# A gate's products as three rounded ones, and a projection's weights loaded after the recurrence

## The chip, the cores and the metric

The kernel runs on one core of a Trainium2 chip. The metric is the device time of one execution in microseconds (us).

## The reference, cut to what matters

One transformer block with 512 tokens of width 1024: a mixer with two branches, then a mixture of experts.

```python
p = h @ w_in                                     # h: 512 x 1024
q, k, v, rw_cols, gate_logits = split(p)
y_sb = stick_breaking_attention(q, k, v)         # 512 x 512
y_rw = rwkv7_time_mix(rw_cols, ...)              # 512 x 512, a recurrence over the tokens
g_sb, g_rw = split(sigmoid(gate_logits + gate_bias))   # 512 x 1024 each
merged = g_sb * (y_sb @ w_o_sb) + g_rw * (y_rw @ w_o_rw)
x = x + gt1 * rmsnorm(merged @ w_out, gain)
# then: h = rmsnorm(x)...; x = x + gt2 * rmsnorm(experts(h), gain)
```

The change touches the logits of the second gate, `h @ w_in[:, gate columns of g_rw]`, and the projection `y_rw @ w_o_rw`.

## The kernel before

Everything is laid out by hand: each engine has its own list of instructions, and they wait for one another on counting semaphores. Values are kept transposed, with features on the 128 partitions and the 512 tokens along the free axis. `arena` is 17 slots of 128x2048 float32, `ring` has three places of 128x4096 for weights on their way, and tensors of other names (`h_upper`, `wo1_upper`, ...) are laid over the same memory, so that one slot has many tenants in turn. Slots 15 and 16 hold `hT`, the transposed h, in 8 pieces of 128x512 (KD = 8). Slots 0, 1 and 4 hold the tokens of the recurrence, slots 3, 7 and 14 its small matrices.

**Weights** come over the queue of SP in the order of `chunk_table`; each chunk has a place and waits until the chunk that had the place before is used up (`used_by`). GR0 to GR3 are four chunks of 1 MB of gate weights, each for two tiles of 128 columns, in halves of the ring's second place, where `w_o_sb` (OSB) was before. `w_o_rw` (two loads of 1 MB, `load_orw`) goes into two arena slots, just ahead of GR2. WO1 and WO0 are the halves of w_out.

**Two kinds of product.** Most products are full precision: float32 on both sides. Others are written as three products of rounded operands (type fp32r): a value is the sum of an upper part, rounded by a copy into fp32r (ScalarE for weights and h, GpSimd for w_o_rw), and a lower part, value minus upper part (a subtraction on GpSimd or VectorE), and the product is upper x upper + lower x upper + upper x lower. The first projections (L1550 to L1552), the w_o_rw products (L1877 to L1879) and the output products (L1908 to L1910) are made so. The gates (L1656) are full precision.

**The order around the change:**

- Attention with the products of the first gate (GS), then the 64x64 triangular inverses of the recurrence's 8 chunks, with the attention output (w_o_sb, L1667, read out by ScalarE at L843) as filler. Its last product frees the place of GR0 and GR1.
- The start states: products L1798, copied out by ScalarE (L862), the first of them copied on by VectorE to `Zs` (L1222).
- The recurrence, 8 chunks in order (`for cc in range(NCH)`). In each, TensorE forms the z products (L1816), VectorE adds (L1226), TensorE forms the sa products (L1823), ScalarE copies them (L879), TensorE forms outputs and the next state (L1841, L1849), VectorE updates the state (L1235, L1238) and ScalarE copies the outputs (L883). Ahead of each of three of these steps stands `gate_part`, two of the GR products, six in a chunk: 48 of the 64. ScalarE reads out each finished gate tile (`gate_evac`, L873).
- The tail: a group norm over each head (sums L1855 and L1862 on TensorE, squares, logarithm and exponential L895 to L899 on ScalarE, L1242 to L1248 on VectorE), with the last 16 GR products between and behind L1862. Then y is rounded (ScalarE, L902) and its lower part formed (VectorE, L1251), GpSimd rounds and splits the second half of w_o_rw (L580, L582), and TensorE forms the w_o_rw products, output tile by output tile (f = 0 to 7, four k in each).
- VectorE multiplies by the gates and adds (L1262, L1263), the sum is split (L914, L1256), w_out is split (ScalarE L908, GpSimd L587), the output products follow in two halves of four token tiles, ScalarE squares each bank (L923, L927), then comes the norm, the router, and a loop over the experts, whose weights (w_up, w_down) SP loads.

The wait at the head of the w_o_rw products is for each k of the first tile: its lower part of y and its parts of w_o_rw.

Of the kernel before, what the change touches and what calls it, by code (L numbers as in the profile page):

```python
# [20 lines left out]
P = 128  # L21
# [96 lines left out]
def build(nc, x, c, w_mod, b_mod, gains, w_in, gate_bias, shift_mu, w0, w_decay_up, a0, w_iclr_up, w_gate_up,  # L118
# [3 lines left out]
    with ctx:  # L122
# [20 lines left out]
        with (nc.sbuf_tensor("over0", [P, 4096], F32), nc.sbuf_tensor("wo0_lower", [P, KD, 512], F32R) as wo0_lower,  # L143
              nc.sbuf_tensor("over1", [P, 4096 + 1024], F32), nc.sbuf_tensor("m_upper0", [P, 6, 512], F32R) as m_upper0,
              nc.sbuf_tensor("over2", [P, 7 * 2048], F32), nc.sbuf_tensor("wo0_upper0", [P, 4, 512], F32R) as wo0_upper0,
              nc.sbuf_tensor("over3", [P, 2048], F32), nc.sbuf_tensor("wo0_upper1", [P, 4, 512], F32R) as wo0_upper1,
              nc.sbuf_tensor("over4", [P, 2048], F32), nc.sbuf_tensor("m_upper1", [P, 2, 512], F32R) as m_upper1,
              nc.sbuf_tensor("over5", [P, 3072], F32), nc.sbuf_tensor("wo1_upper", [P, KD, 512], F32R) as wo1_upper):
            pass
        with (nc.sbuf_tensor("on0", [P, 3 * 4096 + 2 * 2048], F32), nc.sbuf_tensor("orw_upper0", [P, 2, D], F32R) as orw_upper0,  # L150
              nc.sbuf_tensor("on1", [P, 5 * 2048], F32), nc.sbuf_tensor("orw_upper1", [P, 2, D], F32R) as orw_upper1,
              nc.sbuf_tensor("on2", [P, 2048], F32), nc.sbuf_tensor("y_lower", [P, FT, T], F32R) as y_lo,
              nc.sbuf_tensor("on3", [P, 3 * 2048], F32), nc.sbuf_tensor("orw_lower1", [P, 2, D], F32R) as orw_lower1):
            pass
# [35 lines left out]
        def S4(i):  # L190
# [14 lines left out]
        s_orw = (11, 14)  # L205
# [8 lines left out]
               for i in (s_MT, s_X, s_XT, s_Mak, s_Mrb, s_Mrk, s_W, s_B, s_Kd)}  # L214
# [17 lines left out]
        m_hi = [m_upper0[:, k, :] for k in range(6)] + [m_upper1[:, k, :] for k in range(2)]  # L232
        m_lo = [w_parts[:, :, :, :, :].rearrange("p a b k n -> p (a b k n)")[:, 512 * k:512 * k + 512] for k in range(KD)]
        wo_hi = [[wo1_upper[:, k, :] for k in range(KD)],
                 [wo0_upper0[:, k, :] for k in range(4)] + [wo0_upper1[:, k, :] for k in range(4)]]
# [134 lines left out]
        orw_hi = [orw_upper0[:, k, :] for k in range(2)] + [orw_upper1[:, k, :] for k in range(2)]  # L370
        orw_lo = [wo0_upper1[:, 2 * k:2 * k + 2, :].rearrange("p a n -> p (a n)") for k in range(2)]
        orw_lo += [orw_lower1[:, k, :] for k in range(2)]
        W_SPLIT, H_SPLIT, H_ROUNDED = len(proj_tiles) + FT, KD // 2 + FT, KD + FT
# [49 lines left out]
        def load_orw(eng):  # L423

            eng.wait_ge(hp_done, 4)
# [8 lines left out]
        def _(sp):  # L434
            sp.wait_ge(params_in, 16 * N_SMALL)
            for n, (name, src, width, sl) in enumerate(chunk_table):
# [14 lines left out]
                if name == "GR2":  # L451
                    load_orw(sp)
                if name == "WO1":
                    sp.wait_ge(yc_done, NCH)
                    sp.wait_ge(zc_evac, NCH)
                if name == "WO0":
                    sp.wait_ge(sb_gated, KD)
                    sp.wait_ge(rows_moved, 16)
                    for m in range(4):
                        if m in (0, 3):  # L460
                            sp.dma_start(rows[:, 0, :] if m == 0 else row_out, mod_dram[m, :].partition_broadcast(P)).then_inc(rows_moved, 16)
# [6 lines left out]
            sp.wait_ge(mix_done, 4 * KD)  # L468
            load_expert(sp, 1, 0, 1)
# [68 lines left out]
        def _(pool):  # L538
# [35 lines left out]

            pool.wait_ge(orw_in, 32)
            for k in range(FT):
                if k == 2:
                    pool.wait_ge(yc_done, NCH)
                whole_k = orw[k // 2][:, k % 2, :]
                nc.gpsimd.tensor_copy(orw_hi[k], whole_k).then_inc(h_split[0], 1)  # L580
                pool.wait_ge(h_split[0], KD // 2 + k + 1)
                nc.gpsimd.tensor_tensor(orw_lo[k], whole_k, orw_hi[k].bitcast(F32), ALU.subtract).then_inc(w_split, 1)  # L582

            def output_weight_lower(half, k):

                pool.wait_ge(w_rounded, len(proj_tiles) + KD * half + k + 1)
# [7 lines left out]
            nc.gpsimd.memset(S(14), 0.0)  # L594
            nc.gpsimd.memset(S(13)[:, D:2 * D], 0.0).then_inc(hrow_zero, 1)
            pool.wait_ge(merged_ready, KD)
            nc.gpsimd.memset(none, 0.0).then_inc(hrow_zero, 1)

            pool.wait_ge(hrow_zero, 1)
# [53 lines left out]
        def _(act):  # L653
# [203 lines left out]

            for b in range(4):
# [9 lines left out]
            act.dma_start(mod_dram.rearrange("m (f p) -> (m f) p", p=P), prow[0:32, :]).then_inc(rows_moved, 16)  # L868

# [19 lines left out]

            act.dma_start(x1[:, :, :], x.rearrange("o (t p) n -> p (o t) n", p=P)).then_inc(x_in, 16)  # L890
# [113 lines left out]
        def _(dve):  # L1004
# [211 lines left out]
            PCv = PC[:, :].rearrange("p (f c) -> p f c", c=NCH)  # L1216
            f4 = lambda a: a.rearrange("p (f v) -> p f v", f=FT)
            pairs = lambda a: a.rearrange("p (g b v) -> p g b v", b=2, v=HD)
            for cc in range(NCH):
                if cc == 0:  # L1220
                    dve.wait_ge(hp_evac, 8)
                    CP(Zs[:, :], tok[s_H][:, 0, :, :].rearrange("p f v -> p (f v)")).then_inc(zc_evac, 1)  # L1222
                else:
# [25 lines left out]
            for f in range(FT):  # L1249
                dve.wait_ge(h_rounded, KD + f + 1)  # L1250
# [212 lines left out]
        def _(pe):  # L1463
# [180 lines left out]
            def gate(branch, n, ks, bank):  # L1644
# [10 lines left out]
                for k in ks:  # L1655
# [211 lines left out]
            for f in range(KD):  # L1867
# [4 lines left out]
                for k in range(FT):  # L1872
                    if f == 0:
                        pe.wait_ge(h_split[1], KD // 2 + k + 1)
                        pe.wait_ge(w_split, len(proj_tiles) + k + 1)
# [188 lines left out]
```

## Time and profile before

| | us |
|---|---|
| median of 3 runs (lowest, highest) | 1157.81 (1157.76 to 1158.61) |
| profiled execution, own time | 1158.76 |
| its span | 1157.0 |
| TensorE busy | 1019.7 (88%) |
| TensorE loading weights | 540.0 (47%) |
| VectorE busy | 399.9 (35%) |
| ScalarE busy | 275.7 (24%) |
| GpSimd busy | 207.9 (18%) |
| mean granted clock of TensorE, share of full | 0.97 |

The busy times are unions over one profiled execution, so an engine's share is an average over stages with different limits. PE is TensorE, PEld its weight loads, DVE VectorE, ACT ScalarE, POOL GpSimd, SP the engine whose queue issues the loads. The records of the tile names are those of the memory, so a name can be that of another tenant.

### The profile page before, as it was taken

How to read it: one execution, taken by the hardware profiler on the slowest of the kernel's cores; microseconds unless marked ns; L12 is line 12 of the kernel's file. 1: busy time of each engine (PE TensorE's matmuls, PEld its weight loads, DVE VectorE, ACT ScalarE, POOL GpSimd, SP SyncE). 2: the span in 40 equal slices, each digit the busy share in tenths (PEclk: the TensorE clock that was granted, in tenths of full speed). 3: DMA queues.
4: the chain of work that ended last, by engine and by line, in shares of the span. 5: the costliest groups of instructions: out<-in, count | busy, mean ns of one | idle time of the engine just before them, and what ended most of it. 6: DMA issues, size and time to landing. Idle time of an engine off the chain costs nothing.

```text
span 1157.0 us, 16874 instructions
## 1 busy us (share of the span) xinstructions
PE 1019.7 (88%) x7002; PEld 540.0 (47%) x7002; DVE 399.9 (35%) x822; ACT 275.7 (24%) x435; POOL 207.9 (18%) x246
## 2 busy tenths in 40 slices
PE   3899999999998999999998799987777778878886
PEld 1578644465555676555886433333223232323231
DVE  1322466455557443115726412211111111111014
ACT  2343350066552222216433000000000000000004
POOL 0345200003330100102710121111111111111002
PEclk9599999999999999999999799999999999899999
DMA  8434314343322002314527999999999999999995
GB/s 326 158 123 149 106 40 145 139 152 110 109 73 74 3 4 76 111 38 178 208 106 284 343 399 401 393 397 405 406 410 405 406 406 411 392 400 402 412 412 226
DMA packets 71186, 281.67 MB, mean 243 GB/s; under 512 B 9754, under 2 KB 19244, under 8 KB 46554
## 3 DMA queue, kind: packets, MB, share of 16 engines
q1 hardware_dynamic: 63408, 265.94, 59.3%
q0 software_dynamic: 5120, 8.40, 2.3%
q10 hardware_dynamic: 2602, 6.52, 1.5%
q8 instruction: 43, 0.70, 0.3%
q14 instruction: 13, 0.11, 0.0%
HBM read 276.62 MB, written 12.60 MB: 250 GB/s over the span
## 4 chain that ended last, share of the span: by engine, by line
PE 49%; SPq 30%; DVE 7%; DMA 7%; ACT 4%; issue 2%; POOL 1%; ACTq 0%; POOLq 0%; DVEq 0%
SPq L410 21%; PE ps L1656 7%; SPq L414 5%; PE ps L1537 5%; PE ps L1978 4%; SPq L418 3%; PE ps L1550 2%; PE ps L1667 2%; DMA ring<-in_w_up 2%; PE ps L1551 2%; PE ps L1552 2%; PE ps L1582 2%; PE ps L1993 2%; DMA ring<-in_w_mod 2%; PE ps L1766 1%
## 5 line engine op out<-in xcount | busy, mean ns | idle before, releaser
L1978 PE MATMUL ps<-arena 128*64 128x512 f32 x672 | 151.8, 596 | 34.9 <-DMA arena<-in_w_up 34.9
L1423 DVE TENSOR_TENSOR arena<-arena,ps 128x256 f32<-128x256 f32 x32 | 13.5, 421 | 371.1 <-ACT arena L961 371.1
L1656 PE MATMUL ps<-arena,ring 128*128 128x512 f32 x256 | 118.6, 604 | 0.2 <-DMA ring<-in_w_in 0.2
L1978 PEld LDWEIGHTS ps<-arena 128*64 128x64 f32 x672 | 48.9, 137 | 136.4 <-issue 105.2
L1993 PE MATMUL ps<-arena 128*64 128x512 f32 x336 | 83.4, 641 | 19.4 <-DMA arena<-in_w_down 14.8
L1978 PE MATMUL ps<-ring,arena 128*64 128x512 f32 x352 | 80.5, 601 | 14.8 <-DMA ring<-in_w_up 14.8
L961 ACT ACTIVATE arena<-ps 128x256 f32<-128x256 f32 x32 | 12.3, 384 | 259.4 <-PE ps L1978 259.4
L1656 PEld LDWEIGHTS ps<-arena,ring 128*128 128x128 f32 x256 | 46.1, 190 | 49.1 <-issue 47.2
L1418 DVE TENSOR_SCALAR arena<-ps,par 128x64 f32<-128x64 f32 x256 | 67.2, 334 | 4.1 <-PE ps L1967 4.1
L558 POOL TENSOR_SCALAR_AFFINE_SELECT arena<-arena 128x128 f32<-128x128 f32 x64 | 32.4, 540 | 186.3 <-DVE arena L1149 168.5
L968 ACT ACTIVATE arena<-ps 128x512 f32<-128x512 f32 x32 | 19.1, 597 | 187.8 <-PE ps L1993 187.8
L629 POOL COPY dst_now<-dst_i 128x1 int32 x27 | 4.8, 178 | 300.5 <-ACT arena L968 300.5
L1978 PEld LDWEIGHTS ps<-ring,arena 128*64 128x64 f32 x352 | 26.8, 138 | 66.7 <-issue 39.1
L1993 PEld LDWEIGHTS ps<-arena 128*64 128x64 f32 x336 | 26.4, 146 | 61.9 <-issue 44.9
L1537 PE MATMUL ps<-arena,ring 128*128 128x512 f32 x128 | 55.1, 592 | 0.0
L1993 PE MATMUL ps<-ring,arena 128*64 128x512 f32 x176 | 43.6, 641 | 11.0 <-DMA ring<-in_w_down 8.7
L542 POOL TENSOR_TENSOR w_parts<-ring,w_parts 128x1024 fp32r<-128x1024 f32 (+1 forms) x15 | 38.6, 2578 | 80.8 <-ACT w_parts L701 80.8
L1550 PE MATMUL ps<-h_upper,w_parts 128*128 128x512 f32 (+1 forms) x120 | 48.1, 401 | 4.4 <-ACT arena L709 4.4
L1551 PE MATMUL ps<-h_lower,w_parts 128*128 128x512 f32 (+1 forms) x120 | 47.8, 398 | 0.0
L1552 PE MATMUL ps<-h_upper,w_parts 128*128 128x512 f32 (+1 forms) x120 | 47.7, 397 | 0.0
L1967 PEld LDWEIGHTS ps<-cst,arena 64*128 64x128 f32 x256 | 30.7, 201 | 32.1 <-issue 32.1
L1967 PE MATMUL ps<-cst,arena 64*128 64x64 f32 x256 | 35.0, 278 | 5.4 <-DMA arena<-h_rows,idx_i 5.4
(377 smaller groups left out, 1584.1 us busy)
## 6 DMA issues: line engine op xcount, KB each, us to landing
arena<-in_w_up SPq DMA_DIRECT2D x84, 1024.0 KB, 28.9
ring<-in_w_up SPq DMA_DIRECT2D x44, 1024.0 KB, 28.8
ring<-in_w_down SPq DMA_DIRECT2D x11, 2048.0 KB
arena<-in_w_down SPq DMA_DIRECT2D x11, 2048.0 KB, 32.3
ring<-in_w_mod SPq DMA_DIRECT2D x10, 2048.0 KB, 9.1
arena<-in_w_down SPq DMA_DIRECT2D x20, 1024.0 KB
ring<-in_w_in SPq DMA_DIRECT2D x6, 2048.0 KB, 8.4
ring<-in_w_in SPq DMA_DIRECT2D x8, 1024.0 KB, 9.0
```

The lines of the kernel that those rows point to most:

```text
L410: eng.dma_start(eset_up[u][i][:, 2048 * m:2048 * m + 2048], src).then_inc(w_in_sem[u][m], 16)
L414: eng.dma_start(dst, src).then_inc(w_in_sem[u][m], 16)
L542: nc.gpsimd.tensor_tensor(w_parts[:, n % 2, 1, :, 0:w], chunk(name, KD)[:, :, a:a + w], w_parts[:, n % 2, 0, :, 0:w].bitcast(F32), ALU.sub ...
L1418: last = TS(hgT[:, k, :], ps[:, 0, CAP * k:CAP * k + CAP], V("A1", k), V("SH1", k), ALU.mult, ALU.add)
L1537: last = mm(ps[0:m_, b, :], w[:, k, a:a + m_], hT[:, k, :], start=(k == 0), stop=(k == KD - 1))
L1550: mm(ps[0:m_, b, :], hi, h_hi[:, k, :], start=(k == 0), stop=False)
L1551: mm(ps[0:m_, b, :], hi, h_lo[:, k, :], start=False, stop=False)
L1552: last = mm(ps[0:m_, b, :], lo, h_hi[:, k, :], start=False, stop=(k == KD - 1))
L1656: last = mm(ps[:, bank, :], w[:, k, P * (n % 2):P * (n % 2) + P], hT[:, k, :], start=(k == 0), stop=(k == KD - 1))
L1967: last = tr(ps[:, 0, CAP * k:CAP * k + CAP], hv[:, k, :], ident[0:CAP, 0:CAP])
L1978: last = mm(ps[64 * hf:64 * hf + 64, UP_BANK[u], :].rearrange("p (m n) -> p m n", m=2), hgT[:, k, :], up_pair(u, k)[:, :, 256 * hf:256 * h ...
L1993: last = mm(ps[64 * hf:64 * hf + 64, DOWN_BANK[u], :], hv2[:, k % 2, k // 2, :], wd[:, k % 2, 512 * hf:512 * hf + 512], start=(k == 0), st ...
```

## The change

1. The products of the second gate, 64 in full precision, become 192 rounded ones. The first gate (GS) stays.
2. h is split once more: ScalarE rounds its 8 rows into `g_upper0` and `g_upper1` (slots 11 and 14), four before the start states are copied out and four after it; the lower parts overwrite `hT`, even rows on GpSimd, odd ones on VectorE around the copy of Zs.
3. The gate weights are split tile by tile: ScalarE rounds 128x1024 into one of two halves of slot 2, GpSimd subtracts in place. Tiles 0 and 1 are rounded around the start states, tile n+2 after tile n is read out. GpSimd makes all of these ahead of its work on w_o_rw.
4. `w_o_rw` goes to slots 0 and 1, which the recurrence uses to its end. It is loaded behind the waits for the end of the recurrence, ahead of WO1. GpSimd rounds and splits all four parts after that.
5. x is loaded a second time after the w_o_rw products and no longer when the recurrence has ended; the first of the late rows is loaded there too. The clearing of slot 14 follows the output products.

The core of the diff (memory overlays, renumbered waits and places left out):

```diff
                 if name == "AQ":
...
-                if name == "GR2":
-                    load_orw(sp)
                 if name == "WO1":
                     sp.wait_ge(yc_done, NCH)
                     sp.wait_ge(zc_evac, NCH)
+                    load_orw(sp)
...
             sp.wait_ge(mix_done, 4 * KD)
+            sp.dma_start(rows[:, 0, :], mod_dram[0, :].partition_broadcast(P)).then_inc(rows_moved, 16)
             load_expert(sp, 1, 0, 1)
...
+            def gate_rows_lower(k):
+                pool.wait_ge(h_rounded, KD + k + 1)
+                nc.gpsimd.tensor_tensor(g_lo[k], hT[:, k, :], g_hi[k].bitcast(F32), ALU.subtract).then_inc(h_split[0], 1)
+            def gate_weight_lower(n):
+                pool.wait_ge(w_rounded, len(proj_tiles) + n + 1)
+                at = slice(P * (n % 2), P * (n % 2) + P)
+                nc.gpsimd.tensor_tensor(gw_lo[n // 2 % 2][:, :, at], chunk(f"GR{n // 2}", KD)[:, :, at], gw_hi[n % 2].bitcast(F32),
+                                        ALU.subtract).then_inc(w_split, 1)
+            gate_rows_lower(0)
+            gate_rows_lower(2)
+            gate_weight_lower(0)
+            gate_rows_lower(4)
+            gate_rows_lower(6)
+            for n in range(1, KD):
+                gate_weight_lower(n)
             pool.wait_ge(orw_in, 32)
+            pool.wait_ge(yc_done, NCH)
             for k in range(FT):
-                if k == 2:
-                    pool.wait_ge(yc_done, NCH)
                 whole_k = orw[k // 2][:, k % 2, :]
                 nc.gpsimd.tensor_copy(orw_hi[k], whole_k).then_inc(h_split[0], 1)
...
             act.wait_ge(dve_chunk, 8)
+            def gate_rows_upper(k):
+                A(g_hi[k], hT[:, k, :], ACT.Copy).then_inc(h_rounded, 1)
+            def gate_weight_upper(n):
+                arrived(act, f"GR{n // 2}")
+                if n >= 2:
+                    act.wait_ge(mix_done, 2 * KD + n - 1)
+                A(gw_hi[n % 2], chunk(f"GR{n // 2}", KD)[:, :, P * (n % 2):P * (n % 2) + P], ACT.Copy).then_inc(w_rounded, 1)
+            for k in range(4):
+                gate_rows_upper(k)
+            gate_weight_upper(0)
             for b in range(4):
...
+            for k in range(4, KD):
+                gate_rows_upper(k)
+            gate_weight_upper(1)
...
                         gate_evac(n)
-            act.dma_start(x1[:, :, :], x.rearrange("o (t p) n -> p (o t) n", p=P)).then_inc(x_in, 16)
+                        gate_weight_upper(n + 2)
...
-                if k == 4:
+                if k == 0:
                     act.wait_ge(mix_done, 4 * KD)
+                    act.dma_start(x1[:, :, :], x.rearrange("o (t p) n -> p (o t) n", p=P)).then_inc(x_in, 16)
...
-                for k in ks:
+                if branch == "GR":
+                    cols = slice(P * (n % 2), P * (n % 2) + P)
+                    if ks[0] == 0:
+                        pe.wait_ge(w_split, len(proj_tiles) + n + 1)
+                    for k in ks:
+                        if n == 0:
+                            pe.wait_ge(h_rounded, KD + k + 1)
+                            pe.wait_ge(h_split[k % 2], KD // 2 + k // 2 + 1)
+                        mm(ps[:, bank, :], gw_hi[n % 2][:, k, :], g_hi[k], start=(k == 0), stop=False)
+                        mm(ps[:, bank, :], gw_hi[n % 2][:, k, :], g_lo[k], start=False, stop=False)
+                        last = mm(ps[:, bank, :], gw_lo[n // 2 % 2][:, k, cols], g_hi[k], start=False, stop=(k == KD - 1))
+                for k in ks if branch == "GS" else ():
                     last = mm(ps[:, bank, :], w[:, k, P * (n % 2):P * (n % 2) + P], hT[:, k, :], start=(k == 0), stop=(k == KD - 1))
```

## Rows read from the trace of the kernel before

**Rows 1.** The page: busy share of the DMA engines in 40 slices, and the chain by line.

```profile
DMA  8434314343322002314527999999999999999995
...
SPq L410 21%; PE ps L1656 7%; SPq L414 5%; PE ps L1537 5%; PE ps L1978 4%; SPq L418 3%; PE ps L1550 2%; PE ps L1667 2%; DMA ring<-in_w_up 2%; PE ps L1551 2%; PE ps L1552 2%; PE ps L1582 2%; PE ps L1993 2%; DMA ring<-in_w_mod 2%; PE ps L1766 1%
```

**Rows 2.** Timeline of one step of the recurrence, VectorE and TensorE: start, duration, engine, line.

```profile
500.58 0.43 DVE L1226 TENSOR_TENSOR SDZ<-ps,arena 128x256 f32<-128x256 f32 x1 [1.97 <-PE ps L1816]
...
502.36 0.46 PE L1823 MATMUL ps<-SDZ,arena 64*64 64x64 f32 x15
```

**Rows 3.** Timeline of TensorE: first gate products, the tail, the fourth w_o_rw product.

```profile
458.73 3.70 PE L1656 MATMUL ps<-arena,ring 128*128 128x512 f32 x8 [0.24 <-DMA ring<-in_w_in]
...
532.02 1.02 PE L1862 MATMUL ps<-arena,cst 128*128 128x512 f32 x2
...
532.88 11.32 PE L1656 MATMUL ps<-arena,ring 128*128 128x512 f32 x26
...
546.10 0.39 PE L1877 MATMUL ps<-wo_upper,orw_upper 128*128 128x512 f32 x1
```

**Rows 4.** Timeline of ScalarE in the output stage: one square for each bank.

```profile
577.49 0.60 ACT L923 ACTIVATE arena<-ps 128x512 f32<-128x512 f32 x1 [4.18 <-PE ps L1910]
...
582.93 0.60 ACT L923 ACTIVATE arena<-ps 128x512 f32<-128x512 f32 x1 [4.42 <-PE ps L1910]
```

**Rows 5.** Timeline at the start of the recurrence: SP's queue and ScalarE.

```profile
451.65 1.25 SPq L464 DMA_DIRECT2D ring<-in_w_in  x2
...
451.66 0.60 ACT L843 ACTIVATE raw<-ps 128x512 f32<-128x512 f32 x1 [0.45 <-PE ps L1667]
...
457.69 2.32 ACT L862 ACTIVATE arena<-ps 128x256 f32<-128x256 f32 x8 [5.43 <-PE ps L1798]
```

**Rows 6.** Groups by line: ScalarE's rounding (busy us, mean ns).

```profile
L701 ACT ACTIVATE w_parts<-ring 128x1024 fp32r<-128x1024 f32 x14 | 14.6, 1048 | 20.3 <-DMA ring<-in_w_in 20.3
...
L908 ACT ACTIVATE wo_upper<-arena 128x512 fp32r<-128x512 f32 x8 | 4.9, 618 | 0.0
```

**Rows 7.** Timeline of GpSimd: two weight tiles split, the second half of w_o_rw.

```profile
38.82 4.67 POOL L542 TENSOR_TENSOR w_parts<-ring,w_parts 128x1024 fp32r<-128x1024 f32 x2 [38.33 <-ACT w_parts L701]
...
522.53 1.04 POOL L580 CAST orw_upper<-arena 128x1024 fp32r<-128x1024 f32 x1 [28.49 <-PE ps L1849]
...
525.94 1.05 POOL L580 CAST orw_upper<-arena 128x1024 fp32r<-128x1024 f32 x1
```

**Rows 8.** DMA issues: count, KB each, median us to landing.

```profile
arena<-in_w_o_rw SPq DMA_DIRECT2D x2, 1024.0 KB, 6.7
```

**Rows 9.** Timeline of VectorE in the group norm, GpSimd at rest.

```profile
529.69 0.69 DVE L1246 TENSOR_TENSOR arena<-arena 128x512 f32<-128x512 f32 x1 [1.94 <-ACT arena L899]
...
538.40 2.49 DVE L1251 TENSOR_TENSOR y_lower<-arena,wo_upper 128x512 fp32r<-128x512 f32 x4
```

**Rows 10.** Timeline: GpSimd alone, then both engines at once.

```profile
546.95 1.29 POOL L587 TENSOR_TENSOR h_lower<-arena,wo_upper 128x512 fp32r<-128x512 f32 x1 [17.51 <-ACT wo_upper L908]
...
567.50 3.49 DVE L1256 TENSOR_TENSOR w_parts<-ring,m_upper 128x512 fp32r<-128x512 f32 x2
...
568.85 3.30 POOL L587 TENSOR_TENSOR wo_lower<-ring,wo_upper 128x512 fp32r<-128x512 f32 x2
```

**Rows 11.** Timeline of TensorE: returns after idle time (in brackets).

```profile
371.27 0.98 PE L1702 MATMUL ps<-arena 64*64 64x128 f32 x14 [3.25 <-DVE arena L1197]
...
647.85 1.12 PE L1967 MATMUL ps<-cst,arena 64*128 64x64 f32 x8 [5.37 <-DMA arena<-h_rows,idx_i]
```

**Rows 12.** Windows: busy us of PE, PEld, DVE, ACT, POOL; granted clock, DMA share, GB/s.

```profile
365.00:372.00 7.00, 3.75 (x22) 1.73 (x22) 6.97 (x11) 0.83 (x2) 0.00 (x0) 1.00 0.00 0
647.00:652.00 5.00, 4.15 (x26) 3.87 (x28) 2.11 (x8) 0.19 (x1) 1.17 (x2) 0.50 0.69 221
652.00:657.00 5.00, 5.00 (x23) 3.06 (x21) 0.00 (x0) 0.41 (x1) 0.00 (x0) 0.89 1.01 378
```

**Rows 13.** DMA issues: the loads of x.

```profile
arena<-in_x ACTq DMA_DIRECT2D x2, 2048.0 KB, 10.3
```

More of the change, by code:

```diff
@@ L204, in build @@
         s_H, s_y, s_y2 = 6, 10, 12
-        s_orw = (11, 14)
+        s_orw = (0, 1)
         s_rows, s_x1 = 0, 3
@@ L231, in build @@
         squares = S(12, 1)[:, 1024:2048]
-        m_hi = [m_upper0[:, k, :] for k in range(6)] + [m_upper1[:, k, :] for k in range(2)]
+        m_hi = [g_upper0[:, k, :] for k in range(4)] + [g_upper1[:, k, :] for k in range(4)]
         m_lo = [w_parts[:, :, :, :, :].rearrange("p a b k n -> p (a b k n)")[:, 512 * k:512 * k + 512] for k in range(KD)]
         wo_hi = [[wo1_upper[:, k, :] for k in range(KD)],
-                 [wo0_upper0[:, k, :] for k in range(4)] + [wo0_upper1[:, k, :] for k in range(4)]]
+                 [wo0_upper0[:, k, :] for k in range(4)] +
+                 [orw_lower[:, 2 + k // 2, 512 * (k % 2):512 * (k % 2) + 512] for k in range(4)]]
         wo_lo = [[h_lo[:, k, :] for k in range(KD)], [wo0_lower[:, k, :] for k in range(KD)]]
@@ L369, in build @@
         y_hi = [wo0_upper0[:, k, :] for k in range(FT)]
[L370 to L373, printed above, removed]
+        orw_hi = [h_hi[:, 2 * k:2 * k + 2, :].rearrange("p a n -> p (a n)") for k in range(FT)]
+        orw_lo = [orw_lower[:, k, :] for k in range(FT)]
+        g_hi, g_lo = m_hi, wo_hi[0]
+        gw_hi = [gw_upper[:, i, :, :] for i in range(2)]
+        gw_lo = [wo0_lower[:, 4 * i:4 * i + 4, :].rearrange("p a n -> p (a n)").rearrange("p (k n) -> p k n", k=KD) for i in range(2)]
+        W_ROUNDED, W_SPLIT = len(proj_tiles) + KD, len(proj_tiles) + KD + FT
+        H_SPLIT, H_ROUNDED = KD + FT, 2 * KD + FT
         def used_by(n):
@@ L423, in load_orw @@
         def load_orw(eng):
-            eng.wait_ge(hp_done, 4)
             wsrc = w_o_rw.rearrange("o (k p) n -> p (o k) n", p=P)
@@ L458, in _ @@
                     sp.wait_ge(rows_moved, 16)
-                    for m in range(4):
-                        if m in (0, 3):
-                            sp.dma_start(rows[:, 0, :] if m == 0 else row_out, mod_dram[m, :].partition_broadcast(P)).then_inc(rows_moved, 16)
+                    for m in range(1, 4):
+                        if m == 3:
+                            sp.dma_start(row_out, mod_dram[m, :].partition_broadcast(P)).then_inc(rows_moved, 16)
                         else:
@@ L1216, in _, with gate_rows_lower @@
             PCv = PC[:, :].rearrange("p (f c) -> p f c", c=NCH)
+            def gate_rows_lower(k):
+                dve.wait_ge(h_rounded, KD + k + 1)
+                TT(g_lo[k], hT[:, k, :], g_hi[k].bitcast(F32), ALU.subtract).then_inc(h_split[1], 1)
             f4 = lambda a: a.rearrange("p (f v) -> p f v", f=FT)
@@ L1220, in _ @@
                 if cc == 0:
+                    for k in (1, 3):
+                        gate_rows_lower(k)
                     dve.wait_ge(hp_evac, 8)
                     CP(Zs[:, :], tok[s_H][:, 0, :, :].rearrange("p f v -> p (f v)")).then_inc(zc_evac, 1)
+                    for k in (5, 7):
+                        gate_rows_lower(k)
                 else:
```

34 lines of the change are left out of this document (15 added, 19 removed).

## The prediction, made before the changed kernel was timed

> **What bounds the kernel now.** I read the page first. Its chain of waits puts 21% of the span on the issue of expert loads, and its DMA line stands at 9 tenths from the 23rd slice on [rows 1]: the expert loop at the end streams weights as fast as they come. That stream begins after the output products, so whatever moves those products moves the end one for one. Before them TensorE sets the pace. The timeline of the recurrence shows it: chunk by chunk there are small products on the state and, between them, products of the second gate (GR) that fill the time in which VectorE and ScalarE copy the state. A wait for them would have to outlast the filler, and none does: VectorE has finished L1226 at 501.01 (500.58 + 0.43) while TensorE comes to the products that need it only at 502.36 [rows 2]. So the recurrence lasts as long as its TensorE work, and a shorter filler makes it shorter.
>
> **What a product costs.** One full-precision product is two records. In the timeline of the tail, one of L1862 takes from 532.02 to 532.88, 0.86 us; the 26 records of GR behind it (13 products) take 11.32 with the overhang of the last, so 0.857 each and an end at about 544.0 [rows 3]. In the output stage ScalarE squares a bank every 5.44 us (577.49, 582.93), and a bank is 24 rounded products there, so 0.227 each and 0.68 for three [rows 4]. Each of the 64 GR products saves 0.177 us. The smallest step between two state waits is two products, 1.71 us before and 1.36 after; VectorE's step above would still be done 1.0 us ahead (501.01 against 502.0). So the 48 products inside the recurrence give 48 x 0.177 = **-8.5 us**. The 16 behind it would give -2.8, if nothing else is late there.
>
> **The start of the recurrence.** GR0 is loaded into the place of w_o_sb, so its load is issued only when the last attention output is done, at 451.65, and it lands just before TensorE's first GR product at 458.73 [rows 3, 5]. Now that product also needs the weights split. ScalarE is free at 452.3 (451.66 + 0.60 [rows 5]) and rounds four rows of h (0.62 each, as L908 does for 512 columns [rows 6]) until 454.8, then waits for GR0 in its order. From 458.5: 1.05 us of rounding 128x1024 (L701 [rows 6]) and 2.34 of subtraction on GpSimd (4.67 for two, L542 [rows 7]) bring the first product to 462.1: **+3.4 us**. Queued behind ScalarE's wait are the copies L862 of the start states: they ran at 457.69 for 2.32 us [rows 5] and now end at 462.0, and VectorE's copy of Zs right after, while TensorE needs it only after two filler steps (464.8): hidden. ScalarE then rounds rows 4 to 7 and the second weight tile, some 3.6 us behind about 0.9 of small work, until 466.5, and the first SAs copy comes 0.2 later than TensorE wants it: **+0.2**. Later tiles are cheap: tile n+2 is rounded when tile n is read out, and its 3.4 us of splitting lie beside all of tile n+1, some 9 us; without that cover each would cost 3.4. GR2 and GR3 no longer queue behind w_o_rw, so they come earlier. The recurrence thus ends 3.4 + 0.2 - 8.5 = **4.9 us earlier**.
>
> **The tail is where it turns.** Count from the end of the recurrence E, 522.4 in the trace (GpSimd, which waits for it, starts at 522.53 [rows 7]). Before, half of w_o_rw was split during the recurrence, and the other half took GpSimd from E+0.1 to E+7.0. Now SP issues w_o_rw only at E. Its two loads, 6.7 us each from issue [rows 8] and one behind the other, land at about E+9, and then all four parts are to be split: one pair of rounding and subtraction is 3.41 us (522.53 to 525.94), four are 13.7. VectorE meanwhile has the group norm: L1246 starts at 529.69 (E+7.3) and L1251 ends at 540.89 (E+18.5) [rows 9], 11.2 us of work in 16 instructions, of which each reads two tensors of SBUF. Before, GpSimd was idle in that stretch. Now both want SBUF at once.
>
> The trace shows what that does. Alone, L1251 takes 2.49 us for four [rows 9], 0.62 each, and one L587 takes 1.29. Where they meet, two L1256 of the same size take 3.49, and two L587 take 3.30 [rows 10]: 1.75 and 1.65 a piece, which is one of either engine added up, less 0.15 to 0.25. They take turns. VectorE starts 0.6 later than before, E+7.9, because ScalarE has the last weight tile (1.05) ahead of the squares and had some 0.45 of idle time in them. If they took no time from each other, the last part of w_o_rw would be there at E+22.7 and y's last lower part at E+19.1. With turns: from E+9.35 the eight instructions of GpSimd alternate with eight of VectorE, 13.7 + 8 x 0.7 - 8 x 0.15 = 18.1, to E+27.4; then VectorE's last two of the norm (1.5) and the four lower parts (2.5): E+31.4. TensorE can start its first w_o_rw product when the first of those is done, E+29.6, and at 0.68 each its fourth at E+31.8. Which engine goes first hardly matters: the sum of both, 7.9 + 11.2 + 13.7, is due before the first output tile can close. Before, the fourth started at 546.10, E+23.7 [rows 3]. So **+8.1 us**, and the -2.8 of the 16 products is swallowed: TensorE would be through with GR at E+19.1 (544.0 is E+21.6, less 2.8, and 0.3 for the later squares) and stand idle for 10.5 us.
>
> The Trainium skill (SBUF — State Buffer, section Who interferes with whom) says that a VectorE instruction with two SBUF inputs and a GpSimd one that reads SBUF exclude each other for the whole instruction, so that the full durations add up. By that rule the fourth product starts near E+32.7 in place of E+31.8, a sum of 1164.5; the rows show the overlap of 0.15 and decide.
>
> **The clock after the idle time.** After an idle stretch of 5.4 us TensorE comes back at 647.85, and the granted clock is 0.50 from 647 to 652 and 0.89 from 652 to 657, so the lower level (1.2 GHz) holds until about 653.1, 5.2 us after the return. After 3.25 us of idle time at 371.27 it stayed at 1.00 [rows 11, 12]. The new stretch is 10.5 us: I take 5.2 us at half speed, **+2.6 us**; the bounds are 0 and 5.2. The idle time at the start is 3.6 us, nearer to the row that stayed at 1.00: I take 0 there, and up to 2.6 for the bound. The Trainium skill (TensorE: Matmul & The Clock Gate, section Why this matters for your kernels) warns of idle gaps between bursts of matmuls, after which the clock falls to its lower level; by it the start would pay too, a sum of 1166.2.
>
> **Moved for nothing.** x is loaded again only after the w_o_rw products, as is the first row of the late rows, behind 2 MB of expert weights. A 2 MB load of x takes 10.3 us to land [rows 13]; with 6.5 MB on the way at once I expect some 17 us, against 26 to the first use in the second half of the output (its four earlier uses can wait). The cover is the idle DMA of the 21st slice, at 2 tenths [rows 1]; without it, it would cost what is over. WO1 starts behind w_o_rw (E+9) and lands near E+16, ScalarE reaches it at E+34. WO0 waits for the last GR tile, which is earlier than before. The clearing of slot 14 goes behind the last output product and has over 20 us until the gather; 0 to 1 us for its use of SBUF, taken as 0.
>
> **Sum.** -8.5 + 3.4 + 0.2 + 8.1 + 2.6 = +5.8 us. The profiled execution took 1158.76 us (span 1157.0 and 1.8 around it), so 1164.6; the median of the runs lies 0.95 below that, so I predict **1163.6 us**.
>
> **The rivals.** (1) As forecast, chance 0.42, with 1161.5 to 1165.5 of its own. (2) The clock falls at the start as well: +2.6, 1166.2; for it speaks that idle stretch of 3.6 us, against it row 371.27; 0.18. (3) No clock loss after the long stretch, because VectorE's short steps pace the first tile: 1161.0; 0.12. (4) The other side, faster: VectorE and GpSimd do not hold each other up in the tail. Then w_o_rw is ready at E+22.8, the fourth product starts 0.9 earlier than before, TensorE's idle time is too short for the clock, and the sum is -4.9 - 0.9 = -5.8, 1152.0. The point from which it decides is the fourth product at E+28.6: earlier than that, the change gains. Against it stand the rows on turns; 0.12. (5) Turns on only about half of the instructions: fourth product near E+27.5, -1.1, with some clock loss up to +1.5: 1156.7 to 1159.3; 0.16, of which 0.05 faster, 0.07 the same, 0.04 slower. That the change doesn't do what it says (three rounded products not cheaper) has next to no chance: the same shapes stand in the output stage.
>
> Within 0.2% (2.3 us) is about what a measurement of this kernel can't tell from no change. Faster: 0.12 + 0.05 = 0.17; same 0.07; slower 0.42 + 0.18 + 0.12 + 0.04 = 0.76. The range is 1155 to 1168: it leaves out rival 4 and the ends of the others, under 2 in 10.
>
> **What would show it.** Right: GR records of 0.227 us; first GR product near 462; the end of the recurrence near 517.5; L1246 to L1251 stretched from 11 to over 20 us with GpSimd's w_o_rw parts between them; a TensorE gap of 10 us or so before the w_o_rw products, at clock 0.50 behind it. Wrong: VectorE's durations stay at 0.7 in the norm beside a busy GpSimd; or w_o_rw lands much earlier than E+9 and is split before the norm begins; or a wait of TensorE for x or the late rows behind it.

## The result, and the profile after

The changed kernel takes 1165.94 us (median of 4 runs, 1165.12 to 1166.29); beside it, in the same session, the kernel before took 1158.21 (4 runs, 1157.76 to 1159.89). The ratio is 1.0063 [1.0046, 1.0081], so the change costs 7.7 us by the medians, and 5.3 to 9.4 by the ends of the interval (0.0046 and 0.0081 of 1158). The forecast was 1163.6, +5.8, and slower: the direction came out, and the size within 2.3 us of the median. The terms did not: one of them is missing in the recurrence, and the tail is smaller than forecast. The profiled execution took 1165.78, its span is 1164.0 (before 1157.0).

The page, first lines of its parts 1 and 2:

```profile
PE 1009.2 (87%) x7066; PEld 554.8 (48%) x7066; DVE 414.8 (36%) x826; ACT 287.4 (25%) x451; POOL 234.6 (20%) x258
...
DMA  8443304443321002116175999999999999999995
```

TensorE is busy for 10.5 us less than before (1019.7), and the kernel is slower: the work taken away stood beside something. VectorE and GpSimd are busy for 15 and 27 us longer; some of that is work, the rest is instructions held up. The expert stream (the row of nines, as in [rows 1]) begins with the same shape, only later.

**The start of the recurrence**, timeline of the changed kernel (start, duration, engine, line; idle time before it in brackets); it answers to [rows 5] and the first of [rows 3]:

```profile
452.02 1.25 SPq L462 DMA_DIRECT2D ring<-in_w_in  x2
452.03 0.60 ACT L861 ACTIVATE raw<-ps 128x512 f32<-128x512 f32 x1 [0.45 <-PE ps L1721]
452.65 2.19 ACT L877 ACTIVATE g_upper<-arena 128x512 fp32r<-128x512 f32 x4
...
459.07 1.06 ACT L884 ACTIVATE gw_upper<-ring 128x1024 fp32r<-128x1024 f32 x1 [4.23 <-DMA ring<-in_w_in]
460.04 2.29 ACT L893 ACTIVATE arena<-ps 128x256 f32<-128x256 f32 x8
460.21 2.35 POOL L583 TENSOR_TENSOR wo_lower<-ring,gw_upper 128x1024 fp32r<-128x1024 f32 x1 [3.50 <-ACT gw_upper L884]
...
462.65 0.65 PE L1706 MATMUL ps<-g_upper,gw_upper 128*128 128x512 f32 x1 [3.78 <-issue]
...
464.38 0.63 PE L1707 MATMUL ps<-wo_upper,gw_upper 128*128 128x512 f32 x1
464.81 0.63 PE L1708 MATMUL ps<-g_upper,wo_lower 128*128 128x512 f32 x1
...
468.13 0.40 PE L1708 MATMUL ps<-g_upper,wo_lower 128*128 128x512 f32 x1
468.36 0.39 PE L1706 MATMUL ps<-g_upper,gw_upper 128*128 128x512 f32 x1
```

The chain is the forecast one: GR0 lands, ScalarE rounds, GpSimd subtracts, TensorE starts at 462.65 after 3.78 us of idle time. The reader should look at the distance of the last two pairs: 0.43 us from product to product at 464, 0.23 at 468. The clock had fallen.

**A wait in the middle of the recurrence**, same timeline. It stands twice, at 482.65 and here:

```profile
508.00 0.69 ACT L907 ACTIVATE ring<-ps,par 128x512 f32<-128x512 f32 x1
...
508.58 1.05 ACT L884 ACTIVATE gw_upper<-ring 128x1024 fp32r<-128x1024 f32 x1
...
509.71 2.46 POOL L583 TENSOR_TENSOR wo_lower<-ring,gw_upper 128x1024 fp32r<-128x1024 f32 x1 [11.72 <-ACT gw_upper L884]
...
512.32 0.47 PE L1706 MATMUL ps<-g_upper,gw_upper 128*128 128x512 f32 x1 [1.21 <-POOL wo_lower L583]
```

ScalarE reads out a finished tile, rounds the weights of the tile after the next, GpSimd subtracts: 4.3 us from 508.00 to 512.32, and TensorE was there at 511.11.

**The windows** of the changed kernel (busy us of PE, PEld, DVE, ACT, POOL; granted clock; DMA share; GB/s). The last is the whole recurrence, from the first gate product to the end:

```profile
460.00:465.00 5.00, 2.35 (x6) 1.90 (x7) 1.26 (x2) 4.59 (x16) 3.74 (x3) 0.78 0.04 12
465.00:470.00 5.00, 5.00 (x84) 3.64 (x86) 2.14 (x2) 1.43 (x3) 4.38 (x2) 0.88 0.00 0
...
547.00:552.00 5.00, 1.73 (x4) 1.44 (x5) 4.93 (x8) 2.95 (x4) 0.00 (x0) 0.50 0.95 366
552.00:557.00 5.00, 5.00 (x17) 3.93 (x17) 1.40 (x3) 2.77 (x4) 1.29 (x1) 0.71 0.01 2
557.00:562.00 5.00, 5.00 (x24) 4.14 (x23) 3.29 (x5) 2.31 (x4) 1.94 (x2) 1.00 0.01 3
462.65:522.59 59.94, 57.52 (x976) 42.72 (x976) 11.02 (x23) 19.67 (x37) 18.08 (x8) 0.97 0.13 38
```

The same window of the kernel before:

```profile
458.73:522.44 63.71, 63.71 (x928) 32.69 (x928) 9.26 (x21) 13.25 (x34) 6.74 (x4) 1.00 0.21 72
```

Read the two together: TensorE starts 3.9 us later, needs 3.8 less, and ends 0.15 later. Nothing is gained in the recurrence. Before it had no idle time and full clock; now it has 2.4 us of idle time (the two waits) and 0.97.

**The tail**, timeline of the changed kernel, GpSimd and VectorE; it answers to the last two of [rows 7] and to [rows 9]. E, the end of the recurrence, is 522.6 now:

```profile
530.41 1.04 POOL L598 CAST h_upper<-arena 128x1024 fp32r<-128x1024 f32 x1 [2.89 <-DMA arena<-in_w_o_rw]
...
534.18 1.50 POOL L598 CAST h_upper<-arena 128x1024 fp32r<-128x1024 f32 x1
...
534.71 1.52 DVE L1289 TENSOR_TENSOR arena<-arena 128x512 f32<-128x512 f32 x1
...
535.76 2.72 POOL L600 TENSOR_TENSOR orw_lower<-arena,h_upper 128x1024 fp32r<-128x1024 f32 x1
...
536.26 2.77 DVE L1290 SCALAR_TENSOR_TENSOR arena<-arena,par 128x512 f32<-128x512 f32 x1
...
538.43 1.50 POOL L598 CAST h_upper<-arena 128x1024 fp32r<-128x1024 f32 x1
...
549.53 2.49 DVE L1294 TENSOR_TENSOR y_lower<-arena,wo_upper 128x512 fp32r<-128x512 f32 x4
...
550.27 0.79 PE L1931 MATMUL ps<-wo_upper,h_upper 128*128 128x512 f32 x1 [8.46 <-DVE y_lower L1294]
...
555.57 0.69 DVE L1305 TENSOR_TENSOR arena<-ring,ps 128x512 f32<-128x512 f32 x1 [3.55 <-PE ps L1933]
```

VectorE's steps of the group norm, 0.69 and 0.75 us alone, last 1.41 to 2.86 as long as GpSimd works beside them, and its ends follow GpSimd's: the 2.77 of 536.26 ends at 539.03, 0.6 after GpSimd's 2.72. One period of GpSimd (a rounding and a subtraction, 534.18 to 538.43) is 4.25 us, in which VectorE gets two steps done. The three added up would be 3.41 and 1.44, 4.85; so 0.6 in 4.85 overlaps. TensorE stands idle for 8.46 us, comes back at clock 0.50 (the windows above), and VectorE can use the first output tile at 555.57, 8.5 us later than before (547.08 in the timeline of the kernel before). From there the end is 7.0 later: the last output product's loads (SP L410) go out 7.9 later (624.42 against 616.48), the gather before the experts 6.6.

### The profile page after: what moved, and what is told of

The parts are those of the page before. It is cut to its first block, busy times and chain, and to the rows that moved or that the text cites. A ratio compares the mean times of both kernels' runs of the same rounds, so it can differ in the third digit from the quotient of the medians.

```text
span 1164.0 us, 17050 instructions
## 1 busy us (share of the span) xinstructions
PE 1009.2 (87%) x7066; PEld 554.8 (48%) x7066; DVE 414.8 (36%) x826; ACT 287.4 (25%) x451; POOL 234.6 (20%) x258
## 4 chain that ended last, share of the span: by engine, by line
PE 48%; SPq 29%; DVE 7%; DMA 7%; ACT 5%; issue 3%; POOL 1%; ACTq 0%; POOLq 0%; DVEq 0%
SPq L410 21%; SPq L414 5%; PE ps L1580 5%; PE ps L2032 4%; SPq L418 3%; PE ps L1721 2%; PE ps L1593 2%; DMA ring<-in_w_up 2%; PE ps L1594 2%; PE ps L1595 2%; PE ps L1625 2%; PE ps L2047 2%; DMA ring<-in_w_mod 2%; PE ps L1710 2%; PE ps L1820 1%
## 5 line engine op out<-in xcount | busy, mean ns | idle before, releaser
L1710 PE MATMUL ps<-arena,ring 128*128 128x512 f32 x128 | 56.9, 597 | 0.0
L1580 PE MATMUL ps<-arena,ring 128*128 128x512 f32 x128 | 55.1, 592 | 0.0
L1580 PEld LDWEIGHTS ps<-arena,ring 128*128 128x128 f32 x128 | 24.3, 190 | 30.6 <-issue 30.6
```

Source lines behind the costliest of these rows:

```text
L1580: last = mm(ps[0:m_, b, :], w[:, k, a:a + m_], hT[:, k, :], start=(k == 0), stop=(k == KD - 1))
L1710: last = mm(ps[:, bank, :], w[:, k, P * (n % 2):P * (n % 2) + P], hT[:, k, :], start=(k == 0), stop=(k == KD - 1))
```

## The experiments

The kernel before was run again with each group: 1157.77 us (14 runs) beside the first four, 1159.05 (21 runs) beside the last four. Since it differs between sessions, ratios are compared, and 0.001 is 1.16 us. The changed kernel itself was not run again beside them: a difference between its ratio (1.0063) and another carries both intervals, about 0.0023 either way. The differences of experiments 2 and 3 (0.0024) are at that edge, so these two rest on their traces as much as on their times.

**1. The late load by itself.** The kernel before with only this:

```diff
-                if name == "GR2":
-                    load_orw(sp)
                 if name == "WO1":
                     sp.wait_ge(yc_done, NCH)
                     sp.wait_ge(zc_evac, NCH)
+                    load_orw(sp)
...
             pool.wait_ge(orw_in, 32)
+            pool.wait_ge(yc_done, NCH)
             for k in range(FT):
-                if k == 2:
-                    pool.wait_ge(yc_done, NCH)
```

> The kernel before with one part of the change only: w_o_rw is loaded and split after the recurrence, the gate stays in full precision. My account (splitting on GpSimd and the group norm on VectorE exclude each other, 11.2 + 13.7 us less some overlap): the fourth w_o_rw product starts near 29.5 us after the end of the recurrence in place of 23.7, with an idle stretch of some 5 us on TensorE and perhaps 1.5 us of lower clock behind it: 1163.5 to 1166. If the late load and split are hidden and the loss sits in the gate's own splits: within 1 us of before, 1158 to 1159.

Measured: 1168.12 us, ratio 1.0088 [1.0072, 1.0105]. That is above the range expected, and by the medians no less than what the whole change costs. (The profiled execution is the fastest of the four, 1165.74; in it the fourth w_o_rw product starts at 551.96, 29.9 us after the end of the recurrence, where 29.5 was expected.) So the loss comes with the late load; the rounded gate, on top of it, gave at most some 3 us (the two intervals overlap, so whether it gave anything is not settled by these two). Its loads took longer, since x still goes out beside them: 9.7 us to landing against 6.7 in [rows 8], and GpSimd starts at 534.69. Its timeline shows the same turns in the last part of VectorE's chain, where four y lower parts take 8.50 us instead of 2.49:

```profile
535.12 1.41 DVE L1246 SCALAR_TENSOR_TENSOR arena<-arena,par 128x512 f32<-128x512 f32 x1
536.45 2.84 DVE L1244 TENSOR_TENSOR arena<-arena 128x512 f32<-128x512 f32 x1
...
543.40 8.50 DVE L1249 TENSOR_TENSOR y_lower<-arena,wo_upper 128x512 fp32r<-128x512 f32 x4
```

**2. The turns taken away, the load as late.** The changed kernel, where GpSimd starts on w_o_rw when VectorE is through:

```diff
             pool.wait_ge(orw_in, 32)
-            pool.wait_ge(yc_done, NCH)
+            pool.wait_ge(h_split[1], KD + FT)
```

> The changed kernel, but GpSimd begins to split w_o_rw only when VectorE has made y's last lower part. Exclusion: VectorE's instructions of the norm are back at 0.69 to 0.75 us and end near 541, GpSimd's four pairs take 13.7 from there, the fourth product starts near 554.8 against 553.0 in the changed kernel: 1 to 2.5 us slower than it, 1167 to 1168.5. If VectorE's long durations had another cause (its own waits), they stay long, and the split then comes 13.7 us behind 552: 1177 or more.

Measured: 1168.94, ratio 1.0087 [1.0070, 1.0104], a little above the range expected; the fourth w_o_rw product starts at 555.55 (expected 554.8). The timeline of this kernel, VectorE and GpSimd, has VectorE's steps back at 0.69 and 0.75, GpSimd's at 1.04 and 2.34, and the kernel is no faster:

```profile
538.42 0.75 DVE L1291 SCALAR_TENSOR_TENSOR arena<-arena,par 128x512 f32<-128x512 f32 x1
539.09 2.49 DVE L1294 TENSOR_TENSOR y_lower<-arena,wo_upper 128x512 fp32r<-128x512 f32 x4
...
541.72 1.04 POOL L598 CAST h_upper<-arena 128x1024 fp32r<-128x1024 f32 x1 [13.68 <-DVE y_lower L1294]
542.84 2.34 POOL L600 TENSOR_TENSOR orw_lower<-arena,h_upper 128x1024 fp32r<-128x1024 f32 x1
```

This separates the rule "sum of both engines" from "the turns themselves cost". What counts is the sum of the work that must be done behind E by two engines that hardly overlap; in which order matters little.

**3. Part of it on an engine that doesn't take turns.** ScalarE rounds w_o_rw behind its work on the norm, GpSimd only subtracts:

```diff
-                nc.gpsimd.tensor_copy(orw_hi[k], whole_k).then_inc(h_split[0], 1)
-                pool.wait_ge(h_split[0], KD + k + 1)
+                pool.wait_ge(orw_rounded, k + 1)
...
+            act.wait_ge(orw_in, 32)
+            for k in range(FT):
+                A(orw_hi[k], orw[k // 2][:, k % 2, :], ACT.Copy).then_inc(orw_rounded, 1)
             for f in range(FT):
                 act.wait_ge(yrw_ready, f + 1)
```

> The changed kernel, but ScalarE rounds the four parts of w_o_rw behind its exponentials, and GpSimd only subtracts. Exclusion: 4 x 1.04 us less to be shared, the first w_o_rw product 2 to 3 us earlier: 1163 to 1164. If the end is set by the landing of the load or by anything else than the sum of both engines: no change, 1165 to 1166.

Measured: 1162.85, ratio 1.0039 [1.0025, 1.0054], a little under what was expected. GpSimd's part starts later (536.00, the four subtractions take 10.85), VectorE's last four norm steps still take 2.71 to 2.89 each, and TensorE's idle time is 5.68 us instead of 8.46. Beside ScalarE's rounding (four in 3.89 us, from 534.78) VectorE's steps stay at 0.69 and 0.75 until GpSimd begins: these two engines don't hold each other up here. Taking 4 x 1.04 out of the sum gave 0.0024, 2.8 us.

**4. Nothing to split behind E.** The w_o_rw products in full precision, straight from the late-loaded weights and y; neither is split (the products; the instructions that round and subtract are left out as well):

```diff
-                        pe.wait_ge(h_split[1], KD + k + 1)
-                        pe.wait_ge(w_split, len(proj_tiles) + KD + k + 1)
+                        pe.wait_ge(yrw_ready, FT)
+                        pe.wait_ge(orw_in, 32)
                     at = slice(P * f, P * f + P)
-                    mm(ps[:, f % 4, :], orw_hi[k][:, at], y_hi[k], start=(k == 0), stop=False)
-                    mm(ps[:, f % 4, :], orw_hi[k][:, at], y_lo[:, k, :], start=False, stop=False)
-                    last = mm(ps[:, f % 4, :], orw_lo[k][:, at], y_hi[k], start=False, stop=(k == FT - 1))
+                    last = mm(ps[:, f % 4, :], orw[k // 2][:, k % 2, at], S4(s_y)[:, k, :], start=(k == 0), stop=(k == FT - 1))
```

> The changed kernel with the w_o_rw products in full precision: neither w_o_rw nor y is split. The idle stretch and the lower clock behind it are gone, the 32 products take 27.4 us in place of 21.8, from 541.7: the output products start near 569.2 in place of 574.4: 5 us faster than the changed kernel, 1160 to 1161.5. If the idle stretch is due to the late load and not to the splits, it stays, and the time is above the changed kernel's, 1168 or more.

Measured: 1158.53, ratio 1.0009 [0.9997, 1.0021]: 0.0054 or 6.2 us better than the changed kernel, although its TensorE has 32 x 0.177 = 5.7 us more work. The load is as late as ever. So the late load costs nothing by itself; the splitting that it pushes behind E does. VectorE is undisturbed, and behind the 0.88 us at the head of the norm, which the kernel before has too, TensorE waits for nothing up to the output products. Windows of this kernel:

```profile
522.60:572.00 49.40, 48.96 (x143) 26.97 (x144) 27.22 (x40) 24.85 (x38) 12.85 (x10) 1.00 0.42 141
545.00:550.00 5.00, 5.00 (x13) 2.28 (x12) 2.94 (x5) 1.34 (x3) 1.67 (x2) 1.00 1.00 338
```

The clock stays at 1.00 where it was 0.50. It came out 1.5 us below its expected range: the output products begin at 568.29 and not at 569.2, and the kernel before took 0.4 us less beside it than beside the changed kernel; the rest has no known cause.

The other four look for what the recurrence lost.

**5. GR0 earlier.** The first gate weights go to a free half of the ring's third place, so they need not wait for the attention output, and are split ahead of the rows of h:

```diff
-                        ("GR0", *gate_q[4], 3), ("GR1", *gate_q[5], 4), ("GR2", *gate_q[6], 3), ("GR3", *gate_q[7], 4),
+                        ("GR0", *gate_q[4], 7), ("GR1", *gate_q[5], 4), ("GR2", *gate_q[6], 3), ("GR3", *gate_q[7], 4),
...
+        before[chunk_names.index("GR2")] = chunk_names.index("GR0")
...
+            if slot_of[n] == 7:
+                return ring[:, 2, 2048:4096]
...
+                if name == "GR0":
+                    sp.wait_ge(dve_chunk, 8)
...
+            gate_weight_lower(0)
             gate_rows_lower(0)
             gate_rows_lower(2)
-            gate_weight_lower(0)
...
+            gate_weight_upper(0)
             for k in range(4):
                 gate_rows_upper(k)
-            gate_weight_upper(0)
```

> The changed kernel, but the first chunk of gate weights is loaded early, into the half of the ring that takes the last gate tiles later, and its first tile is rounded ahead of the rows. The idle stretch of 3.8 us at the first gate product goes, and with it 1.65 us of lower clock: 5 to 5.5 us faster than the changed kernel, 1160 to 1161.5. If ScalarE's and GpSimd's row splits alone hold the first product as long: no change.

Measured: 1161.68, ratio 1.0020 [1.0011, 1.0029], 0.0043 or 5.0 us better than the changed kernel, more than the 3.4 of the idle time alone. The clock at the first gate products is what comes on top: they run at full clock from the start (461.15, 461.39, 461.63 in its timeline). A wait of 0.66 us for the lower parts of the rows 4 to 7 appears at 464.92.

**6. Gate weights rounded earlier.** A tile that is finished in the first or second step of a chunk is read out, and the next weights rounded, at once and not at the chunk's end:

```diff
                   ps[:, 4:6, 256:384].rearrange("p b (g v) -> p g b v", v=HD), ACT.Copy).then_inc(sa_evac, 1)
+                for n in range(6):
+                    if (KD * n + KD - 1) // GR_PART == cc and (KD * n + KD - 1) % GR_PART < 4:
+                        gate_evac(n)
+                        gate_weight_upper(n + 2)
                 act.wait_ge(yc_done, cc + 1)
```

> The changed kernel, but gate tiles that are finished in the first two thirds of a chunk are read out, and the tile after next rounded, right behind the SAs copy and no longer at the end of the chunk. The two waits of 1.2 us for GpSimd's lower parts in the third and seventh chunk go: 2.4 us faster, 1163 to 1164. If those waits only take up slack of the state's own chain: no change, 1165.9.

Measured: 1163.18, ratio 1.0035 [1.0021, 1.0049], 0.0028 or 3.2 us better. Both waits of 1.21 us are gone; the only one left is that of the start, 3.65 at 462.26.

**7. Both of them.**

> The two edits together. If the two losses are independent: 7.5 us faster than the changed kernel, recurrence of 56.0 us, total 1157.5 to 1159, about the time before. If one hides the other: 1160.

Measured: 1158.28, ratio 0.9993 [0.9983, 1.0002]. 0.0070 or 8.1 us better than the changed kernel, against 5.0 and 3.2 for each: within the intervals they add up. This version is what the forecast of the recurrence described, together with the tail as it is, and it comes out level with the kernel before.

**8. All three**, 4, 5 and 6 in one kernel.

> The two edits at the start and the w_o_rw products in full precision. TensorE has no wait left from the first gate product to the output products; 64 gate products at 0.68 us and some 0.1 for each change of kind, 32 w_o_rw products at 0.857: 12 to 13 us faster than the changed kernel, 1153 to 1154.5, which is below the time before. If a new wait or the expert loads take the gain: 1158.

Measured: 1153.36 (5 runs, 1152.22 to 1153.87), ratio 0.9946 [0.9933, 0.9960]. It beats both kernels, the one before by 0.54%. Between the first gate product and the output products TensorE has one wait besides the 0.88 us at the head of the norm. The timeline shows it, and the windows the clock there:

```profile
462.44 0.47 PE L1702 MATMUL ps<-g_upper,gw_upper 128*128 128x512 f32 x1 [0.81 <-POOL wo_upper L582]
```

```profile
460.00:465.00 5.00, 4.19 (x92) 3.06 (x90) 3.11 (x3) 3.41 (x6) 3.98 (x3) 1.00 0.01 3
465.00:470.00 5.00, 5.00 (x62) 3.59 (x53) 1.18 (x3) 1.53 (x4) 1.79 (x1) 1.00 0.01 3
```

From the copy of the last attention output to the end of the recurrence it takes 63.5 us (451.43 to 514.93); the changed kernel takes 70.6 (452.03 to 522.59), the one before 70.8 (451.66 to 522.44).

## Why the prediction was right, and which of its terms were not

For the profiled execution the total is right within 1.2 us of a span that grew by 7.0 (1164.6 forecast, 1165.78 measured), and the side is right. It is partly luck: by terms,

| | forecast | measured |
|---|---|---|
| recurrence ends | -4.9 | +0.15 |
| tail, without the clock | +8.1 | +6.5 |
| clock in the tail | +2.6 | +1.9 |
| behind the first output tile | 0 | -1.5 |
| sum | +5.8 | +7.0 |

The tail without the clock is the 8.5 of the first output tile less 0.15 and 1.9; the last row is 7.0 less 8.5.

**The cost of a product: right.** Rounded gate products stand 0.23 us apart at full clock (468.13, 468.36), as 0.227 said.

**The start: right.** TensorE's first gate product was to come at 462.1; it came at 462.65, with everything before it 0.37 late already, so +3.55 where +3.4 was forecast. The copy of Zs was hidden, as said.

**The recurrence: the step that failed.** From the first gate product to the end the forecast has 63.7 - 8.5 + 0.2 = 55.4 us, and it was 59.9. The missing 4.5 are three things:

- 2.4 us: "Later tiles are cheap ... beside all of tile n+1, some 9 us". They are not. A tile that ends in the first step of a chunk is read out only at the end of the chunk, because ScalarE's order has it there. By then half of tile n+1 is done, and TensorE is at the next tile 3.1 us later (508.00 to 511.11), while the chain takes 4.3. It happens for tiles 0 and 3. The prediction took the cover from the length of a tile and not from the place of the instruction in its engine's order. Experiment 6 shows it.
- 1.5 us: the clock fell at the start. Eight products, 463.11 to 466.38, took 3.27 us where 8 x 0.227 is 1.8. This is rival 2 (chance 0.18), at little over half its price: it had taken the 5.2 us at the lower level from the tail's row, and it lasted some 3.4. The choice rested on the row at 371.27 (3.25 us idle, clock 1.00), and one row of one execution was too little: in the last section the same gap has the other outcome. The Trainium skill (TensorE: Matmul & The Clock Gate, section Why this matters for your kernels) warns of such gaps; the trace agrees for this gap of 3.78 us, while the one of 3.25 us at 371 went both ways.
- 0.6 us: the change between gate products and small ones. ScalarE's copies of sa come every 7.10 us in the undisturbed chunks (489.86, 496.97, 504.07, 511.18) and came every 8.08 before (486.72, 494.80). A chunk thus gains 0.98 and not 6 x 0.177 = 1.06, eight times 0.08. In the timeline the first rounded product behind small ones stands 0.34 us ahead of the next, not 0.23 (509.06, 509.40), three times in a chunk. Most of what such a change costs is not new. Two full-precision products between small ones took 1.91 us (500.45 to 502.36), 0.20 more than their own 1.71; six rounded ones take 1.59 (494.85 to 496.44), 0.23 more than their own 1.36. Only the 0.03 is added, three times in a chunk. This part was read and not tested by a run of its own.

They sum to 4.5. The trace of experiment 6, which has no waits but the one at the start, agrees: 57.5 us from the first gate product to the end (462.26 to 519.71), which is 55.4 and the last two of the three. Experiments 5, 6 and 7 give back the waits, the clock and most of the idle time at the start.

**The tail: mechanism right, size a little large.** Both engines' work adds up, as forecast; experiments 2 to 4 show it from three sides (same sum in another order, no gain; less of it, less loss; none of it, no loss). Two things made it smaller. w_o_rw was in use at E+7.8 and not E+9.35 (530.41): its loads, issued from 522.66, took 6.2 us to landing by the row of the DMA issues, and lay more beside each other than the forecast had them. And the overlap of a turn was 0.3 us (0.6 in a period with two of GpSimd's instructions) and not 0.15. VectorE's chain ended at 552.0, E+29.4, where E+31.4 was forecast; a third norm step left over behind the turns gave a little back. The Trainium skill (SBUF — State Buffer, section Who interferes with whom) has such instructions exclude each other for their whole length; here the steady period was 4.25 us and not the 4.85 that this gives, so it is nearer to the rows than no interference (rival 4) is, and still too strict.

**The clock in the tail: right.** TensorE returned after 8.46 us at half clock. From its first w_o_rw product to its twelfth it took 4.78 us (550.27 to 555.05), the kernel before 2.92 (543.63 to 546.55): 1.9, against 2.6.

**The moved loads: right.** They now fall in the output stage (DMA share 0.90 from 580 to 600). VectorE did wait for x, until 595.28, 18 us after its issue at 577.05 (forecast: 17), but TensorE lost nothing by it: it is busy without a break from 575 to 598. The clearing of slot 14 took its 1.80 us at 624.45, and nobody waited for it.

**Behind the first output tile: luck.** The forecast had no term here, and 1.5 us come back. The first output product is 8.5 us later than before (565.82, 574.36), ScalarE's square of the last bank 7.9 (616.49, 624.43): the kernel before waits 0.30 us for VectorE's split at 571.04, the changed one doesn't. The router's last logits are only 6.6 later (624.18, 630.76). Between these the clock falls in the kernel before and not in the changed one, behind the same short gap, in the timelines of the two:

```profile
618.83 1.87 PE L1889 MATMUL ps<-cst,arena 128*128 128x128 f32 x8 [0.68 <-DVE arena L1326]
620.50 1.91 PE L1929 MATMUL ps<-cst 128*128 128x512 f32 x2
```

```profile
626.77 1.23 PE L1943 MATMUL ps<-cst,arena 128*128 128x128 f32 x8 [0.68 <-DVE arena L1369]
627.84 1.02 PE L1983 MATMUL ps<-cst 128*128 128x512 f32 x2
```

The granted clock is 0.50 from 620 to 622 in the first and 1.00 from 626 to 632 in the second. These 1.4 us (7.94 less 6.58) are not the work of the change; they depend on which execution was profiled. Without them this pair of spans would differ by 8.4 us and not 7.0 (the medians differ by 7.7), and the forecast of 5.8 would be further off. Another 0.4 us are lost between there and the end; they were not followed.

## What to carry to other kernels

When an operand's place forces its load to move, count what must be done to it behind the load, on the engines that do it: here the late load was free (experiment 4) and the splitting behind it cost 6 us more than full-precision products that need none. Two engines that take turns on SBUF, as VectorE and GpSimd do in this tail, are one engine for planning; move a part of the work to a third, or do without it. And read the cover of a step from its place in its engine's list to the first instruction that needs the result, not from the length of the work in between: that alone was 2.4 us of waits, and moving the read-out ahead in ScalarE's list gave 3.2 back.

## What the runs showed of the hardware that was not expected

**The same gap costs the clock in one execution and not in the next.** No edit touches the stage around 371, where TensorE waits 3.25 us for VectorE. Its return in the timeline of the changed kernel:

```profile
370.01 3.14 PE L1756 MATMUL ps<-arena 64*64 64x128 f32 x32 [3.25 <-DVE arena L1231]
```

and in that of experiment 8:

```profile
371.04 1.96 PE L1752 MATMUL ps<-arena 64*64 64x128 f32 x32 [3.25 <-DVE arena L1230]
```

The same 32 products take 3.14 us or 1.96, and the ten profiles split in halves: 3.14 here and 2.37 to 3.27 in experiments 2, 5, 6 and 7, with clock 0.72 to 0.86 from 372 to 378; 1.96 in the kernel before and in experiments 1, 3, 4 and 8, with 1.00. A second place is in the profile of experiment 5 (timeline of TensorE, then windows). It has no idle stretch over 0.9 us just before, and yet the clock is at 0.59 during the products of the start states, which take 3.42 us where the kernel before took 2.10:

```profile
455.36 0.28 PE L1845 MATMUL ps<-cst,par 128*32 128x128 f32 x1 [0.84 <-DVE arena L1252]
455.48 2.06 PE L1847 MATMUL ps<-rt,cst 128*128 128x36 f32 x16
457.46 3.42 PE L1857 MATMUL ps<-arena 64*64 64x64 f32 x128
```

```profile
458.00:461.00 3.00, 3.00 (x121) 2.93 (x114) 0.88 (x1) 1.25 (x5) 2.02 (x2) 0.59 0.04 13
```

The profiles of experiments 2 and 7 have both falls as well (0.54 and 0.55 in that window), and that of 7 is the slowest of its ten runs, 1162.14, where the fastest took 1156.16; experiment 8 has the same instructions up to there and neither fall. The third place is the one behind the output products, shown above. Each fall costs 1 to 2 us, so several of them can make the spread of the runs of one kernel (1157.14 to 1161.29 for the kernel before beside experiments 5 to 8); that they do is inferred from one profile for each kernel. What decides between the two outcomes stays open. For a forecast it means a chance and a price for each such gap, and not a yes or no from one row.

**Large products between small ones take about 0.2 us more than their own time**, 0.20 in full precision and 0.23 rounded, as above.

**Turns in numbers.** In the steady turns a GpSimd rounding of 128x1024 takes 1.50 us (1.04 alone), its subtraction 2.7 (2.34 alone), a VectorE step of 128x512 1.4 when it waits for a rounding and 2.75 when it waits for a subtraction (0.69 to 0.75 alone).
